# Opening of a hybrid decoder layer: memory transposes placed between key products, value weights cut along the contraction, first key weights sent from ScalarE's queue

## What is computed

```
y_c = _memory_attention(mq, jnp.einsum('bmd,dw->bmw', mem, w_mem_k),
                            jnp.einsum('bmd,dw->bmw', mem, w_mem_v))
```

## Time and profile before

| | us |
|---|---|
| median of 3 runs | 834.19 |
| lowest and highest | 834.16, 834.86 |
| span of the profiled execution | 832.3 |
| TensorE busy in it | 818.0 (98%) |
| VectorE busy | 503.0 (60%) |
| ScalarE busy | 351.7 (42%) |
| GpSimd busy | 32.5 (4%) |

### The profile page before, as it was taken

One profiled execution on the slowest core, in us unless ns is written; L12 is line 12 of the kernel. 1 busy time (PEld: TensorE's weight loads), 2 busy tenths in 40 slices (PEclk: granted clock), 3 DMA queues, 4 the chain that ended last, 5 costly groups with the idle time before them and its releaser, 6 DMA issues.

```text
span 832.3 us, 10213 instructions
## 1 busy us (share of the span) xinstructions
PE 818.0 (98%) x4111; PEld 695.3 (84%) x4111; DVE 503.0 (60%) x560; ACT 351.7 (42%) x397; POOL 32.5 (4%) x38
## 2 busy tenths in 40 slices
PE   8999999999999999999999999999999999999994
PEld 7989888899888888888888889888888888888883
DVE  3647745567354424414428685986669666956698
ACT  4549343494434223232225035653545345435532
POOL 1110100000001000000000010000000000000005
PEclk9999999999999999999999999999999999999998
DMA  9641313312122322323723407017201810280002
GB/s 311 196 152 52 102 51 102 101 50 94 57 75 88 118 78 98 101 101 101 302 101 97 156 4 250 1 51 263 92 0 51 298 57 0 64 290 1 0 1 101
DMA packets 68215, 87.52 MB, mean 105 GB/s; under 512 B 1581, under 2 KB 51798, under 8 KB 68182
## 3 DMA queue, kind: packets, MB, share of 16 engines
q1 hardware_dynamic: 68182, 87.06, 31.0%
HBM read 84.96 MB, written 2.10 MB: 105 GB/s over the span
## 4 chain that ended last, share of the span: by engine, by line
PE 94%; DVE 4%; issue 1%; DMA 1%; DVEq 0%; SPq 0%; ACT 0%
PE bank L1358 30%; PE bank L1360 30%; PE bank L1359 30%; DVE two L1222 1%; DMA two<-in_mem_dram 1%; PE bank L1572 0%; PE bank L1522 0%; PE bank L1493 0%; PE bank L1640 0%; PE bank L1385 0%; DVE w_lo L808 0%; DVE two L1250 0%; DVE smx L1228 0%; DVE decay L1228 0%; PE bank L1575 0%
## 5 line engine op out<-in xcount | busy, mean ns | idle before, releaser
L1358 PE MATMUL bank<-x_hi,w_hi 128*128 128x512 f32 (+1 forms) x704 | 268.4, 381 | 0.0
L1359 PE MATMUL bank<-x_lo,w_hi 128*128 128x512 f32 (+1 forms) x704 | 267.2, 380 | 0.0
L1360 PE MATMUL bank<-x_hi,w_lo 128*128 128x512 f32 (+1 forms) x704 | 267.2, 379 | 0.0
L803 DVE TENSOR_TENSOR w_lo<-raw,w_hi 128x2048 fp32r<-128x2048 f32 x40 | 91.4, 2290 | 108.0 <-ACT w_hi L511 107.8
L1360 PEld LDWEIGHTS bank<-x_hi,w_lo 128*128 128x128 f32 x704 | 132.4, 188 | 25.0
L1358 PEld LDWEIGHTS bank<-x_hi,w_hi 128*128 128x128 f32 x704 | 132.4, 188 | 24.6
L1359 PEld LDWEIGHTS bank<-x_lo,w_hi 128*128 128x128 f32 x704 | 132.5, 188 | 24.4
L1358 PE MATMUL bank<-w_hi,y_hi 128*128 128x512 f32 (+1 forms) x320 | 121.4, 379 | 0.0
L1360 PE MATMUL bank<-w_hi,y_lo 128*128 128x512 f32 (+1 forms) x320 | 121.1, 378 | 0.0
L1359 PE MATMUL bank<-w_lo,y_hi 128*128 128x512 f32 (+1 forms) x320 | 121.1, 378 | 0.0
L511 ACT ACTIVATE w_hi<-raw 128x2048 fp32r<-128x2048 f32 x40 | 76.4, 1915 | 41.9 <-PE bank L1360 36.8
(11 more groups left out here) (193 smaller groups left out, 847.2 us busy)
## 6 DMA issues: line engine op xcount, KB each, us to landing
raw<-in_w_in_dram SPq DMA_DIRECT2D x28, 1024.0 KB, 5.0
raw<-in_w_up_dram SPq DMA_DIRECT2D x16, 1024.0 KB, 8.5
small<-in_w_down_dram SPq DMA_DIRECT2D x12, 1024.0 KB, 7.1
raw<-in_w_branch_dram SPq DMA_DIRECT2D x6, 1024.0 KB, 5.0
raw<-in_w_o_dram SPq DMA_DIRECT2D x4, 1024.0 KB, 5.0
raw<-in_w_down_dram SPq DMA_DIRECT2D x4, 1024.0 KB, 4.7
two<-in_x_dram SPq DMA_DIRECT2D x2, 1024.0 KB, 11.9
small<-in_w_mem_v_dram SPq DMA_DIRECT2D x2, 1024.0 KB, 12.5
```

What stands on the lines that cost most here:

```text
L803: dve.tensor_tensor(w_lo[:, slot, :], raw[:, r, :], w_hi[:, slot, :].bitcast(F32), ALU.subtract)\
L1358: pe.matmul(dst, a[0], b[0], start=first, stop=False, skip_group_check=goes_on)
L1359: pe.matmul(dst, a[0], b[1], start=False, stop=False, skip_group_check=goes_on)
L1360: return pe.matmul(dst, a[1], b[0], start=False, stop=last, skip_group_check=goes_on)
```

## The change

What it does:

- The four pieces of the first key weights are issued by ScalarE (4 DMA instructions ahead of its first table load) and no longer by SyncE, whose queue keeps the four quarters of `mem` and goes straight on.
- The value weights are loaded in four pieces of 512 KB along the contraction (two blocks of 128 rows, all 512 columns each), `value_landed` 0 to 3, where there were two pieces of 1 MB along the columns. Pieces 0 and 1 are issued ahead of both halves of `x`, pieces 2 and 3 behind them. High and low parts are made piece by piece (128 x 1024).
- TensorE: the second batch of dummy transposes has 10 and stands right behind memory quarter 0; the dummies inside the loop go. Memory quarter j+1 is transposed between the two tiles' products of quarter j. Key tiles 2 and 3 are interleaved by contraction halves. The value products are 48 of 512 columns, in two groups of 24, each behind 16 transposes of `x`.
- ScalarE copies key tiles 0 and 1 ahead of the value weights; the copies of the value tiles come after `hi(4)` and ahead of `hi(5)`.

The diff:

```diff
--- before.py
+++ after.py
@@ -236,7 +236,7 @@
         small_landed = sem("small_landed")
         mem_landed = [sem("mem_landed%d" % j) for j in range(4)]
         front_landed = [sem("front_landed%d" % j) for j in range(6)]
-        value_landed = [sem("value_landed0"), sem("value_landed1")]
+        value_landed = [sem("value_landed%d" % n) for n in range(4)]
         x_landed = [sem("x_landed0"), sem("x_landed1")]
         slab_landed = [sem("slab_landed0"), sem("slab_landed1")]
         x_again = sem("x_again")
@@ -343,9 +343,6 @@
                 part = slice(j * 256, (j + 1) * 256)
                 sp.dma_start(mem_tok[:, :, part], mem[0].rearrange("(b p) d -> p b d", p=P)[:, :, part])\
                     .then_inc(mem_landed[j], 16)
-                part = slice(2 * j, 2 * j + 2)
-                sp.dma_start(raw[:, 0, :].rearrange("p (k c) -> p k c", k=KD)[:, part], wmk[:, part, 0:256])\
-                    .then_inc(front_landed[j], 16)
             for e in range(2):
                 part = slice(e * KD // 2, (e + 1) * KD // 2)
                 sp.dma_start(raw[:, 1, :].rearrange("p (k c) -> p k c", k=KD)[:, part], wmk[:, part, 256:512])\
@@ -355,9 +352,13 @@
                 sp.dma_start(x_tok[:, :, part], x_t[:, :, part]).then_inc(x_landed[e], 16)
 
             for e in range(2):
-                x_load(e)
-                sp.dma_start(raw_v[:, e].rearrange("p (k c) -> p k c", k=KD), wmv[:, :, e * 256:(e + 1) * 256])\
-                    .then_inc(value_landed[e], 16)
+                for n in range(2 * e, 2 * e + 2):
+                    part = slice(2 * (n % 2), 2 * (n % 2) + 2)
+                    sp.dma_start(raw_v[:, e].rearrange("p (k c) -> p k c", k=KD // 2)[:, part],
+                                 wmv[:, 2 * n:2 * n + 2, :]).then_inc(value_landed[n], 16)
+                if e == 0:
+                    x_load(0)
+                    x_load(1)
             for to, rows_of in ((par_rows[0:24], b_gate[0].rearrange("(r p) -> r p", p=P)),
                                 (par_rows[24:36], conv_w[0].rearrange("t (r p) -> (t r) p", p=P)),
                                 (par_rows[36:40], lower_bounds[0].rearrange("(r p) -> r p", p=P)),
@@ -519,6 +520,10 @@
                 act.activation(w_hi[:, slot, part], raw[:, slot, part], ACT.Copy).then_inc(ready, 1)
 
             for j in range(4):
+                part = slice(2 * j, 2 * j + 2)
+                act.dma_start(raw[:, 0, :].rearrange("p (k c) -> p k c", k=KD)[:, part], wmk[:, part, 0:256])\
+                    .then_inc(front_landed[j], 16)
+            for j in range(4):
                 src = aux_of(act, PRO, "t%d" % j).rearrange("p (k m) -> p k m", k=2)
                 act.activation(memt_hi[:, 2 * j:2 * j + 2, :], src, ACT.Copy).then_inc(transposed_hi, 1)
                 part_hi(0, slice(j * WID, (j + 1) * WID), front_landed[j], front_hi if j < 3 else slab_hi)
@@ -526,27 +531,35 @@
             part_hi(1, slice(SLAB // 2, SLAB), front_landed[5], slab_hi)
 
             def value_hi(e):
-                act.wait_ge(value_landed[e], 16)
-                act.activation(w_hi[:, 2 + e, :], raw_v[:, e], ACT.Copy).then_inc(slab_hi, 1)
+                for n in range(2 * e, 2 * e + 2):
+                    part = slice((n % 2) * SLAB // 2, (n % 2 + 1) * SLAB // 2)
+                    act.wait_ge(value_landed[n], 16)
+                    act.activation(w_hi[:, 2 + e, part], raw_v[:, e, part], ACT.Copy)\
+                        .then_inc(slab_hi if n % 2 else front_hi, 1)
 
             def x_parts(ks):
                 for k in ks:
                     act.activation(x_hi[:, k, :], aux_of(act, PRO, "t%d" % (4 + k)), ACT.Copy)\
                         .then_inc(transposed_hi, 1)
 
+            def key_copied(t):
+                act.activation(mem_k[:, t, :], main_of(act, 0, t)[:, 0:M], ACT.Copy).then_inc(main_read[t], 1)
+
+            key_copied(0)
+            key_copied(1)
             value_hi(0)
-            for s in range(4):
-                if s == 2:
-                    x_parts(range(0, 4))
-                    value_hi(1)
-                    x_parts(range(4, KD))
-                    hi(4, 0, 2)
-                elif s == 3:
-                    hi(5, 1, 4)
-                for c in range(2):
-                    src = main_of(act, 0, 2 * s + c)[:, 0:M]
-                    dst = mem_k[:, 2 * s + c, :] if s < 2 else mem_v[:, c, (s - 2) * 256:(s - 1) * 256]
-                    act.activation(dst, src, ACT.Copy).then_inc(main_read[(2 * s + c) % MAIN], 1)
+            key_copied(2)
+            key_copied(3)
+            x_parts(range(0, 4))
+            value_hi(1)
+            x_parts(range(4, KD))
+            hi(4, 0, 2)
+            for c in range(2):
+                act.wait_ge(tile_done, 4 + 2 * (c + 1))
+                for e in (1, 0):
+                    part = slice((1 - e) * 256, (2 - e) * 256)
+                    act.activation(mem_v[:, c, part], bank[c][:, part], ACT.Copy).then_inc(main_read[2 * e + c], 1)
+            hi(5, 1, 4)
             act.wait_ge(lb_diff, 1)
             act.activation(lbw[:, 1, :], lbw[:, 0, :], ACT.Exp).then_inc(lb_exp, 1)
 
@@ -824,8 +837,14 @@
             part_lo(1, slice(0, SLAB // 2), front_hi, 4, front_lo)
             part_lo(1, slice(SLAB // 2, SLAB), slab_hi, 2, slab_lo)
             def value_lo(e):
-                dve.wait_ge(slab_hi, 2 + e + 1)
-                low_of(w_lo[:, 2 + e, :], raw_v[:, e], w_hi[:, 2 + e, :]).then_inc(slab_lo, 1)
+                for n in range(2 * e, 2 * e + 2):
+                    part = slice((n % 2) * SLAB // 2, (n % 2 + 1) * SLAB // 2)
+                    if n % 2:
+                        dve.wait_ge(slab_hi, 2 + e + 1)
+                    else:
+                        dve.wait_ge(front_hi, 4 + e + 1)
+                    low_of(w_lo[:, 2 + e, part], raw_v[:, e, part], w_hi[:, 2 + e, part])\
+                        .then_inc(slab_lo if n % 2 else front_lo, 1)
 
             def x_parts(ks):
                 for k in ks:
@@ -1394,11 +1413,8 @@
             pe.wait_ge(ident_ready, 1)
             keep_busy(10)
             mem_transposed(0)
+            keep_busy(10)
             for j in range(4):
-                if j < 3:
-                    mem_transposed(j + 1)
-                if j < 2:
-                    keep_busy(8 - 4 * j)
                 aux_copied(pe, PRO, "t%d" % j)
                 if j < 3:
                     pe.wait_ge(front_lo, j + 1)
@@ -1411,31 +1427,35 @@
                                    k == 0, k == KD - 1)
                     if j == 3:
                         mm.then_inc(tile_done, 1)
-            for c in range(2):
-                t = begin(0, 2 + c)[:, 0:M]
-                for k in range(KD):
-                    if c == 0 and k == 0:
-                        pe.wait_ge(front_lo, 4)
-                    if c == 0 and k == KD // 2:
-                        slab(1)
-                    mm = three(t, w_part(1, k * 256 + c * P, P), both(memt_hi, memt_lo, ALL, k),
-                               k == 0, k == KD - 1)
-                mm.then_inc(tile_done, 1)
-
-            for s in range(2, 4):
-                if s == 2:
-                    pe.wait_ge(x_landed[0], 16)
-                    x_transposed(range(0, 4))
-                slab(s)
+                    if c == 0 and j < 3:
+                        mem_transposed(j + 1)
+            for h in range(2):
+                if h == 0:
+                    pe.wait_ge(front_lo, 4)
+                else:
+                    slab(1)
                 for c in range(2):
-                    if s == 2 and c == 1:
-                        pe.wait_ge(x_landed[1], 16)
-                        x_transposed(range(4, KD))
-                    t = begin(0, 2 * s + c)[:, 0:M]
-                    for k in range(KD):
-                        mm = three(t, both(memt_hi, memt_lo, ALL, k, slice(c * P, (c + 1) * P)),
-                                   w_part(s, k * 256, 256), k == 0, k == KD - 1)
-                    mm.then_inc(tile_done, 1)
+                    t = (bank[2 + c] if h else begin(0, 2 + c))[:, 0:M]
+                    for k in range(4 * h, 4 * h + 4):
+                        mm = three(t, w_part(1, k * 256 + c * P, P), both(memt_hi, memt_lo, ALL, k),
+                                   k == 0, k == KD - 1)
+                    if h:
+                        mm.then_inc(tile_done, 1)
+
+            for e in range(2):
+                pe.wait_ge(x_landed[e], 16)
+                x_transposed(range(4 * e, 4 * e + 4))
+                for c in range(2):
+                    t = bank[c] if e else begin(0, 4 + c)
+                    for k in range(4):
+                        if c == 0 and k == 0:
+                            pe.wait_ge(front_lo, 4 + e + 1)
+                        if c == 0 and k == 2:
+                            slab(2 + e)
+                        mm = three(t, both(memt_hi, memt_lo, ALL, 4 * e + k, slice(c * P, (c + 1) * P)),
```

(3 more changed lines are left out.)

## The result

The changed kernel takes 836.43 us (median of 7, 835.89 to 836.95), the kernel before 834.08 us (median of 7, 832.59 to 834.86). The ratio is 1.0033, 95% interval 1.0024 to 1.0042: slower, by some 2.4 us. I had forecast 834.7, no change that can be told, with a range to 836.4. The profiled execution of the changed kernel took 836.95 us, the longest of the seven, with a span of 835.2 us (832.3 before).

What follows compares the result with a forecast made beforehand. TensorE, busy 98% of the span, was taken to bound the kernel. Quarters net of the earlier start +1.17 and values -0.64 gave +0.53 us: 834.7 us against a median of 834.19, range 833.7 to 836.4.

Steps and rivals of the forecast that it cites:

- Part 1, the start: Opening up to the first key product: the wait for memory quarter 1 goes, product at 6.88 us, start gains 1.9 us.
- the rival of the shared path: Opening loads: sharing the load path delays memory quarter 0 by up to 0.6 us, 835.3 us; no chance given.
- Part 2, the quarters: Four memory quarters: 3.42 us apart, three TensorE idles of 1.55 us, quarter 3 at 17.44 us, net loss 1.17 us.
- the late bound: Memory quarters: clock rises only at 10.9 us, as before; quarter 3 at 18.15 us, +1.88 us.
- the early rise: Opening: clock rises at 7.5 us, during the first six products, three of which cost 0.21 us.
- Part 3, key tiles 2 and 3: Key products after quarter 3: same 48 products, weights in time, nothing added; `x` transposes 1.17 us later, at 24.72.
- Part 4, the values: Value products: 48 of 512 columns replace 96 of 256, 11.1 us for 11.76, minus 0.64 us.
- Part 5, what is late next: First projection slab: ready about 0.4 us before TensorE wants it at 39.34 us; cost nothing, cover thin.
- The clock did not fall: Rival, memory quarters: the clock falls in the new gaps, 4.43 us per quarter, 839.4 us; chance 0.10.
- ScalarE was not held by its transfers: Rival, opening: four issues at 1.3 us hold ScalarE until 7.2 us, 837.1 us; chance 0.04.
- The gaps did arise: Rival, memory quarters: no gaps arise, quarters come 1.9 us apart, quarter 3 at 12.6, 829.9 us; chance 0.03.

Runs made afterwards that it cites:

- the value part alone: The kernel before with only the value loads, the 48 wide products and ScalarE's new order; key part and queue as before: 833.38 us, ratio 0.9990.
- two runs of 839 us: Two of five runs of the changed kernel with ScalarE's four transfers held until the identity is ready, 0.8 us later; median 836.54 us.

## Why the prediction was wrong

**Part 1, the start: wrong, and the main miss.** I took the delay of memory quarter 0 by the shared load path as 0 and bounded it at 0.6 us; it is 1.3 us at the landing and 1.11 us at the transposes. The bound was bad reasoning: half the difference between two landings says little about two transfers that run at the same time, of which each lands about when both are done (4.75 and 5.2). I had also read the 2.7 us as quarter 0 "alone on the path", which it was not: piece 0 was issued 0.5 us behind it, at 1.24, but on the same queue, and there quarter 0 came first. What this term costs in the end is the 1.4 us by which undoing the queue shortens the kernel; with it undone the kernel is 0.98 us above the one before, near the +0.5 I had forecast. The rest of the part held: 3.2 us after the transposes the first product starts, at 8.06 for 6.88. I had named the rival of the shared path, but priced it at 0.6.

**Part 2, the quarters: mechanism right, three sizes off.** Three gaps on a low part, 1.16, 1.39 and 1.39 us, where I had 1.55 each. The step is 3.50 and not 3.42 us, since I used 0.12 us for the first of six products, which costs 0.20: +0.15 over two steps. And the clock rose at 10.9 in this execution, which I had as the late bound: first step 4.57 us for 3.72, +0.85. With +1.18 of the start that makes 2.18: quarter 3 at 19.62 for 17.44. The delayed quarter and the late rise belong together, since the break at 3.9 us is what the unbroken work from 1.54 on, on which I had built the early rise, was to exclude; I combined them as independent bounds.

**Part 3, key tiles 2 and 3: right.** With quarter 3's products 7.26 for 7.28 us, no wait.

**Part 4, the values: right, size a little off.** 0.55 us for 0.64, and 0.45 in the times of the value part alone. The products cost as I had them (28.54 to 34.12 holds 24 of them, 5.58 us, where I had 5.56). What I had left out is the last step, to the parameter transpose: 41.09 to 41.41 is 0.32 us, where I had 0.227. Before, that step cost 0.21 instead of 0.12, and it stood in the 11.76 us from which I subtracted. *The Trainium skill's formula in "Back-to-back issue gap" (page "TensorE: Matmul & The Clock Gate") would have given 0.12; the trace does not agree with it for this pattern, in which each product loads its own weights: both widths cost some 11 ns more than it says. The Trainium skill gives the formula there for a single product on its own, and for a stream with weight loads about 131 ns at 512 columns; the 227 ns here do not agree with that either.*

**Part 5, what is late next: right.** Slab 4's low part follows the second `x` transposes and no wait stands before the first projection product. Timeline of VectorE:

```profile
38.65 2.29 DVE L816 TENSOR_TENSOR w_lo<-raw,w_hi 128x2048 fp32r<-128x2048 f32 x1 [0.78 <-ACT w_hi L512]
```

It ends at 40.94, 0.65 us before the product at 41.59.

**The sum.** Forecast +0.53, profile +2.78: 1.18 + 0.85 + 0.15 + 0.09 = 2.27 of the 2.25 us of difference. By the medians +2.35.

**The rivals.** The clock did not fall in gaps of 1.4 us in either profile of the changed kernel, and none of its other runs stands out by its time; at 2.1 us it did. So I was right to doubt, and the fall was closer than I thought. *The section of the Trainium skill that I had named, "A second HAM failure mode: psum-queue depth-cycling", has the clock swing under frequent short idles between groups of products. The changed kernel's trace does not agree (no fall with gaps of 1.2 to 1.4 us); the version with the transposes behind both tiles agrees in part, with one fall and one rise (granted clock 0.50 from 14.4 to 27.9 us).* ScalarE was not held by its transfers (2.07 us for four); the 3.28 us that I had set against 0.46 belong to a transfer four times as large. The gaps did arise.

## What to carry to other kernels

Before moving a producer nearer to its consumer in the program, measure the whole chain between them (here 2.7 us over ScalarE and VectorE) and count the work that still covers it (here 6 products, some 0.8 us): transposing one quarter further ahead costs the same instructions and left no gap at all. A second queue does not make the first load arrive sooner if the other's bytes travel with it; keep the load that the first instruction needs alone at the front. A gap early in a kernel is paid twice if it also delays the rise of the clock, so price the two together.

## What was new about the hardware

- Two transfers of 256 KB issued at the same moment on two queues landed at 4.75 and 5.2 us; alternating on one queue, half a microsecond apart, the first landed at 3.45 and the second at 5.1. Over all profiles the first took 2.7 to 3.0 us with one queue and 3.9 to 4.0 with two. Holding the second queue 0.8 us brought the first to 4.25 and the second to 7.2.
- The granted clock reads 1.00 for the first 10 us in every profile here, although products step at half speed until the rise; a fall later in the run is shown in it as 0.50.
- Gaps of 1.4 us between groups of 2.1 us of work left the clock up in every profile taken of such a version (two runs of 839 us were not profiled); in the one profile with gaps of 2.1 us it fell after the first of them, and it took until 27.9 us, 3.4 us after the last gap, to rise again.
- The moment of the first rise moves from run to run by up to 3 us for the same opening and makes up about 1 us of the spread of the times (835.84 and 836.95 for profiles 1.1 us apart at quarter 3). Versions whose TensorE has no gap from 1.5 to 6.5 us spread over 0.4 to 0.8 us, the kernel before over 832.1 to 835.4. The gap alone does not decide the spread: with the transposes ahead and a gap of 0.86 us the eleven runs spread over 0.8 us too.
